# A sparse-expert decoder block: interleaved columns and a VectorE turn for the rest rows, another order at the first block, and no loads for further blocks where there are none

## The chip, the cores and the metric

The kernel runs on one core of one Trainium2 chip. The metric is the device time of one execution in microseconds (us). Three executions of the kernel before took 2183.55, 2186.32 and 2188.81 us.

## The reference, cut to what matters

One decoder block over 1024 tokens of width 1024: two attention mixers, an output projection, then a sparse FFN with 32 experts. Each token goes to 4 experts, so an expert has 128 tokens on average. The change lies in the FFN alone.

```
logits = xf @ router_w + router_b;  top 4 of 32;  gate = softmax(top logits)
for each expert e, over its tokens x (rows of RMSNorm(h)):
    gu  = x @ w_gate_up[e] + b_gate_up[e]            # 1024 -> 2048, fp32
    g   = min(gu[:, :1024], 7);  u = clip(gu[:, 1024:], -7, 7)
    act = (u + 1) * (g * sigmoid(1.702 * g))
    out[token] += (act @ w_down[e] + b_down[e]) * gate
```

## The kernel before, in words

**Stages.** Norm and attention come first, then merge and output projection with routing, then `experts` (from L1870 on), which computes block b for expert b, b = 0 to 31. A block holds up to 160 token rows. The first 128 are the main rows, the 32 behind them the rest rows. An expert with more than 160 tokens gets further blocks (number 32 and on), whose number `nov` is known only on the chip (`further_blocks`, L1958).

**Main rows.** The weights of a block come in 12 slabs of 1 MB (8 of gate and up, 4 of down), issued by SyncE. ScalarE writes the rounded part `w_hi` of each slab (`split_hi`, L2031), VectorE the remainder `w_lo` (`split_lo`, L2298), and TensorE multiplies hi by hi, lo by hi and hi by lo (`gate_up` L2446, `down` L2490). Half of the hidden columns is ready after slab 3, the other after slab 7. They are activated by ScalarE (`swish`) and VectorE (`activate`), turned on TensorE (`turn_hidden`, L2406), and split by ScalarE (`hidden_hi`) and VectorE (`hidden_lo`, L2329).

**Rest rows.** They are multiplied only in an expert with more than 128 tokens (`more` in `multiply`). With 32 rows a product fills only a quarter of TensorE's columns, so four column groups g = 0 to 3 work side by side, each on another quarter of the output columns, in plain fp32 out of the raw slab (`gate_up_rest` L2468, `down_rest` L2507). In PSUM, partitions 32g to 32g+31 hold the 32 rows for the hidden columns of quarter g: 128 adjoining columns of each half. ScalarE and VectorE activate this tile in every block (`swish_rest` L2043, `activate_rest` L2320 and L2322). In a block with rest rows TensorE then turns the two 128x128 tiles (`turn_hidden_rest`, L2414), between slabs 9 and 10, and ScalarE copies the turned tile to `h_rest` (`hidden_rest`, L2056; in every block). `down_rest` reads `h_rest` behind slab 10.

**Rows in and out.** While block b runs, POOL copies the index tables of block b+2 and, once VectorE has turned the rows of block b+1, gathers the rows of block b+2 by five indirect DMAs (`gather`, L2141). VectorE turns them (`turn_x`, `turn_x_rest` L2348), and ScalarE and VectorE split them (`take_x`, L2065 and L2357). At the end of a block ScalarE scales the result (`take_y` L2071, 128x1024; `take_y_rest` L2078, 128x256), and POOL adds both to the output in HBM by an indirect DMA each (`add_rows`, L2148 main, L2151 rest). On POOL the order in a block is: `add_rows(b-1)`, the new index tables, then the gather. For a further block the tables are read back from `slots` in HBM by 25 small DMAs (`load_slots`, L2131 to L2136).

**The two ends of the stage.** At the start VectorE waits for an iota of POOL (`ini`, L2360), runs `split_lo(0, 0)`, and only then turns the gathered rows of block 0 (L2364), which `take_x(0)` needs. At the end VectorE and ScalarE split three slabs of a block 32 and turn its rows, and POOL loads the tables of blocks 32 and 33 and gathers their rows, whether `nov` is above 0 or not; `add_rows(31)` is behind all of this on POOL.

```
turn = pe.wait(hid2_d); transpose(gu[:, 1, 1, a*P:(a+1)*P], hid2[:, a, :], ident)   # a = 0, 1  (L2410 on)
more:  main(8) turn_hidden(1) main(9) turn_hidden_rest main(10) down_rest(8..11) main(11)
```

## Time and profile before

| | |
|---|---|
| three executions | 2183.55, 2186.32, 2188.81 us (median 2186.32) |
| the profiled execution | 2186.8 us, its span 2185.2 us |
| mean granted TensorE clock | 0.985 |
| TensorE busy | 2095.8 us, 96% of the span |
| VectorE, ScalarE, POOL busy | 1609.1, 1323.1, 850.5 us |
| `w_hi` and `w_lo` splits | 387 each: 32 blocks of 12 slabs and 3 more |

The span runs from the first to the last instruction of the core; the profiled execution's own time is 1.6 us longer. A block without rest rows takes about 34.4 us, one with them 46.5 us. 18 of the 32 blocks have rest rows. 387 splits are 32 blocks of 12 and the three that are made ahead for block 32: on this input no further block runs.

### The profile page before, as it was taken

The numbers are of one execution on the slowest core, as the hardware profiler recorded it, in microseconds if no ns is written. First come the engines' busy times: TensorE is split into PE (matmuls) and PEld (weight loads), VectorE is DVE, ScalarE is ACT, GpSimd is POOL, SyncE is SP. The second block draws the span as 40 slices with busy tenths as digits, with TensorE's granted clock in tenths as the row PEclk, the third lists the DMA queues.
The fourth block names the chain that finished last, engine by engine and source line by source line (L and its number), as shares of the span: only waits on it lengthen the run. The fifth ranks groups of instructions, "written<-read, shape, count | busy, mean of one in ns | idle before, by whom it ended". The sixth has DMA issues, their size and how long they took to land.

```text
span 2185.2 us, 38817 instructions
## 1 busy us (share of the span) xinstructions
PE 2095.8 (96%) x13480; PEld 1618.2 (74%) x13481; DVE 1609.1 (74%) x1604; ACT 1323.1 (61%) x1463; POOL 850.5 (39%) x698
## 2 busy tenths in 40 slices
PE   7989999999999997999999999999999999999995
PEld 7867777777777775777777777777887777777774
DVE  4165767676666466897897897898998778777885
ACT  4266675756444224676676676676876566665664
POOL 1120101010066344465665653454645334433376
PEclk9999999999999997999999999999999999999997
DMA  4101212122255538899999998999999899888992
GB/s 154 31 29 46 70 36 71 29 63 62 78 174 195 190 128 299 310 345 331 336 355 340 332 353 314 346 363 350 396 362 366 280 337 333 309 282 304 345 318 69
DMA packets 270040, 515.19 MB, mean 236 GB/s; under 512 B 37733, under 2 KB 80176, under 8 KB 269964
## 3 DMA queue, kind: packets, MB, share of 16 engines
q1 hardware_dynamic: 242308, 469.61, 59.7%
q0 software_dynamic: 20000, 39.16, 7.3%
q10 hardware_dynamic: 7656, 5.44, 0.8%
q8 instruction: 44, 0.72, 0.1%
q14 instruction: 32, 0.26, 0.0%
HBM read 475.83 MB, written 42.45 MB: 237 GB/s over the span
## 4 chain that ended last, share of the span: by engine, by line
PE 55%; POOL 3%; DVE 1%; issue 1%; DMA 1%; ACT 0%; POOLq 0%; DVEq 0%; ACTq 0%
PE ex_gu L2446 30%; PE ex_yp L2490 15%; PE ex_rest L2468 6%; PE ex_rest L2507 3%; POOL ex_xg L2141 1%; POOL ex_nxt_q L2136 1%; DVE ex_wlo L2298 1%; PE ex_tr L2406 1%; PE ex_gu L2406 1%; DMA out_dram<-ex_ytok,ex_piece 1%; PE ex_gu L2433 0%; DMA ex_nxt_q<-slots 0%; POOL out_dram L2148 0%; PE ex_yp L2437 0%; POOL ex_idx L2171 0%
## 5 line engine op out<-in xcount | busy, mean ns | idle before, releaser
L2298 DVE TENSOR_TENSOR ex_wlo<-ex_raw,ex_whi 128x2048 fp32r<-128x2048 f32 x387 | 872.9, 2286 | 138.6 <-ACT ex_whi L2031 132.5
L2031 ACT ACTIVATE ex_whi<-ex_raw 128x2048 fp32r<-128x2048 f32 x387 | 731.5, 1913 | 133.7 <-PE ex_gu L2446 115.0
L2141 POOL DMA_INDIRECT ex_xg<-xn_s,ex_idx x165 | 338.5, 2052 | 400.6 <-DVE ex_xrest L2348 346.8
L2446 PE MATMUL ex_gu<-ex_whi,ex_xhi 128*128 128x512 f32 x1024 | 284.9, 400 | 13.3 <-DVE ex_xlo L2357 13.1
L2446 PE MATMUL ex_gu<-ex_whi,ex_xlo 128*128 128x512 f32 x1024 | 275.5, 391 | 0.0
L2446 PE MATMUL ex_gu<-ex_wlo,ex_xhi 128*128 128x512 f32 x1024 | 274.5, 390 | 0.0
L2446 PEld LDWEIGHTS ex_gu<-ex_whi,ex_xhi 128*128 128x128 f32 x1024 | 186.4, 189 | 69.2 <-issue 21.6
L2446 PEld LDWEIGHTS ex_gu<-ex_whi,ex_xlo 128*128 128x128 f32 x1024 | 192.9, 188 | 41.6
L2446 PEld LDWEIGHTS ex_gu<-ex_wlo,ex_xhi 128*128 128x128 f32 x1024 | 192.6, 188 | 41.1
L742 POOL TENSOR_TENSOR at_wlo<-at_raw,at_whi 128x1024 fp32r<-128x1024 f32 x15 | 36.1, 2404 | 451.4 <-ACT at_whi L555 451.4
L58 PE MATMUL at_job<-xnT_hi,at_whi 128*128 128x512 f32 x416 | 178.6, 429 | 5.2 <-DVE at_nxt_qa L778 2.9
L60 PE MATMUL at_job<-xnT_hi,at_wlo 128*128 128x512 f32 x416 | 164.3, 395 | 0.0
L59 PE MATMUL at_job<-xnT_lo,at_whi 128*128 128x512 f32 x416 | 163.6, 393 | 0.0
L2490 PE MATMUL ex_yp<-ex_whi,ex_hhi 128*128 128x512 f32 x512 | 147.0, 409 | 0.0
L2490 PE MATMUL ex_yp<-ex_whi,ex_hlo 128*128 128x512 f32 x512 | 137.8, 391 | 0.0
L2490 PE MATMUL ex_yp<-ex_wlo,ex_hhi 128*128 128x512 f32 x512 | 137.7, 391 | 0.0
L2468 PE MATMUL ex_rest<-ex_raw,ex_xrest 128*32 128x256 f32 x2304 | 135.7, 381 | 0.0
L2490 PEld LDWEIGHTS ex_yp<-ex_whi,ex_hlo 128*128 128x128 f32 x512 | 96.2, 188 | 21.5
L2490 PEld LDWEIGHTS ex_yp<-ex_wlo,ex_hhi 128*128 128x128 f32 x512 | 96.2, 188 | 21.3
L2490 PEld LDWEIGHTS ex_yp<-ex_whi,ex_hhi 128*128 128x128 f32 x512 | 89.7, 188 | 28.9 <-issue 11.1
L2468 PEld LDWEIGHTS ex_rest<-ex_raw,ex_xrest 128*32 128x32 f32 x2304 | 70.5, 110 | 53.3 <-issue 12.7
L643 ACT ACTIVATE at_probT<-at_tr 128x512 f32<-128x512 f32 (+1 forms) x120 | 63.2, 527 | 75.9 <-PE at_tr L1022 75.7
(379 smaller groups left out, 3494.6 us busy)
## 6 DMA issues: line engine op xcount, KB each, us to landing
ex_raw<-in_w_gate_up_dram SPq DMA_DIRECT2D x512, 512.0 KB, 8.3
ex_raw<-in_w_down_dram SPq DMA_DIRECT2D x256, 512.0 KB, 8.0
at_raw<-in_w_in_dram SPq DMA_DIRECT2D x25, 512.0 KB
gT<-at_gst SPq DMA_DIRECT2D x32, 256.0 KB, 2.3
mg_g<-gT SPq DMA_DIRECT2D x32, 256.0 KB, 3.9
raw_o<-in_w_out_dram SPq DMA_DIRECT2D x8, 512.0 KB, 5.6
op_x<-in_x_dram SPq DMA_DIRECT2D x8, 512.0 KB, 4.1
out_dram<-op_h SPq DMA_DIRECT2D x8, 512.0 KB, 2.8
```

What stands on the lines that cost most here:

```text
L58: nc.tensor.matmul(out, w_hi, x_hi, start=first, stop=False)
L59: nc.tensor.matmul(out, w_hi, x_lo, start=False, stop=False)
L60: return nc.tensor.matmul(out, w_lo, x_hi, start=False, stop=last)
L643: nc.scalar.activation(probT[:, slot(u), 4 * g:4 * g + n, :].rearrange("p a c -> p (a c)"), tr[:, 0:n * P], ACT.Copy).then_inc(tr_ev, 1)
L2031: nc.scalar.activation(w_hi[:, i % RING, :], raw[:, i % SLABS, :], ACT.Copy).then_inc(hi_d, 1)
L2141: pool.indirect_dma_start(out=xg[:, a, :], out_offset=None, in_=xn_s.rearrange("t (q c) -> (t q) c", q=Q), in_offset=bass.IndirectOffsetOn ...
L2298: nc.vector.tensor_tensor(w_lo[:, slot, :], raw[:, i % SLABS, :], w_hi[:, slot, :].bitcast(F32), ALU.subtract).then_inc(lo_d, 1)
L2406: last = nc.tensor.transpose(dst[:, k * P:(k + 1) * P], hid[:, (4 * half + k) * P:(4 * half + k + 1) * P], ident[:, :])
L2446: mm = nc.tensor.matmul(gu[:, half, h, :], x[:, k, :], w[:, kk, h, :], start=half == 0 and k == 0 and n == 0, stop=k == KD - 1 and n == 2)
L2468: mm = nc.tensor.matmul(part(g), x_rest[:, k, :], gate_up_slab(raw, i)[:, kk, :, g * P:(g + 1) * P], start=k == 0, stop=k == KD - 1)
L2490: mm = nc.tensor.matmul(yp[:, nh, :], x[:, k, :], w[:, kk, nh * HALF:(nh + 1) * HALF], start=False, stop=k == KD - 1 and n == 2)
L2507: mm = nc.tensor.matmul(part(g), h_rest[:, k, :], down_slab(raw, i)[:, kk, g * XW:(g + 1) * XW], start=k == 0, stop=k == KD - 1)
```

## The change

- **Rest rows.** The column groups take interleaved columns. Group g reads, of every 128 columns, the 32 from 32g on: 8 runs of 32 floats for each product of 256 columns, where it read 2 runs of 128. Then each 32x32 piece of `hid2` turned in its place is a piece of `h_rest`. VectorE does that with one transpose of 128x256, in every block, behind `activate_rest`. TensorE's `turn_hidden_rest` and ScalarE's `hidden_rest` are gone, and `down_rest` waits for VectorE.
- **First block.** VectorE no longer waits for `ini`. It turns the gathered rows and does `take_x(0)` before `split_lo(0, 0)`, `split_lo(0, 1)` and the turn of the rest rows.
- **Further blocks.** The rows, tables and slab splits for block 32 are prepared inside `If(nov > 0)` (`begin_further`). The last block prepares nothing.
- **Last output.** The last `take_y` is shared: ScalarE takes columns 0 to 511, VectorE 512 to 1023. `add_rows` issues the rest rows' DMA first, before it waits for the main rows.

The diff, cut to its core:

```diff
@@ further_blocks
+        def further_blocks(eng, body, begin=None):
             with eng.If(nov > 0):
+                if begin is not None:
+                    begin()
@@ scalar
-            def hidden_rest(b):
-                act.wait_ge(h_tr, 3 * b + 3)
-                src = gu[:, 1, 1, 0:2 * P].rearrange("p (k c) -> p k c", k=KD)
-                nc.scalar.activation(h_rest[:, :, :], src, ACT.Copy).then_inc(hh_d, 1)
+            def take_y_half(b):
+                act.wait_ge(slab_mm, SLABS * b + SLABS + RING)
+                act.wait_ge(cur_d, b + 1)
+                nc.scalar.activation(ytok[:, 0:HALF], yp[:, 0, :], ACT.Copy, scale=cur[:, 0, 1:2].bitcast(F32)).then_inc(y_ev, 1)
                 hidden_hi(b, 1)
-                take_x(b + 1)
-                hidden_rest(b)
-                for i in range(12, SLABS + AHEAD):
-                    split_hi(b, i)
+                if not last:
+                    take_x(b + 1)
+                    for i in range(12, SLABS + AHEAD):
+                        split_hi(b, i)
-            body(NE - 1, True)
-            nov = further_blocks(act, body)
-            take_y(nov + (NE - 1))
+            body(NE - 1, False, last=True)
+            nov = further_blocks(act, body, begin_further)
+            take_y_half(nov + (NE - 1))
@@ gpsimd
-            def add_rows(b):
-                hold(pool, y_ev, b + 2, spare)
+            def add_rows(b, parts=1):
                 hold(pool, y2_ev, b + 2, spare)
...
+                hold(pool, y_ev, b + 1 + parts, spare)
...
+            def begin_further():
+                pool.wait_ge(tok_out, 16 * NT * TOPK)
+                next_rows(NE, on_chip=False, late=1)
+                advance(NE + 1)
+                next_rows(NE + 1, on_chip=False)
@@ vector
                 nc.vector.scalar_tensor_tensor(out=hid2[:, :, :], in0=sg2[:, :, :], scalar=SWISH_CAP, in1=hid2[:, :, :],
                                                op0=ALU.min, op1=ALU.mult).then_inc(hid2_d, 1)
+                dve.wait_ge(hid2_d, 2 * b + 2)
+                nc.vector.transpose(h_rest[:, :, :], hid2[:, :, :].rearrange("p a (k c) -> p (a k) c", c=CAP2)).then_inc(hid2_d, 1)
-            dve.wait_ge(ini, 1)
-            split_lo(0, 0)
             for a in range(Q):
                 dve.wait_ge(*landed[max(a - 1, 0)])
                 last = nc.vector.transpose(x_t[:, :, a * CAP2:(a + 1) * CAP2], pieces[:, :, a, :])
             last.then_inc(x_tr, 2)
             take_x(0)
+            for i in range(2):
+                split_lo(0, i)
             dve.wait_ge(*landed[Q - 1])
             turn_x_rest(0)
+            def take_y_half(b):
+                dve.wait_ge(slab_mm, SLABS * b + SLABS + RING)
+                dve.wait_ge(cur_d, b + 1)
+                nc.vector.tensor_scalar(ytok[:, HALF:D], yp[:, 1, :], cur[:, 0, 1:2].bitcast(F32), None, ALU.mult).then_inc(y_ev, 1)
@@ tensor
-            def turn_hidden_rest(b):
-                pe.wait_ge(hid2_d, b + 2)
-                for a in range(2):
-                    last = nc.tensor.transpose(gu[:, 1, 1, a * P:(a + 1) * P], hid2[:, a, :], ident[:, :])
-                last.then_inc(h_tr, 1)
+                his = lambda w, g: w.rearrange("p h (n q c) -> p h n q c", q=Q, c=CAP2)[:, :, :, g, :]
                         mm = nc.tensor.matmul(part(g), x_rest[:, k, :],
-                                              gate_up_slab(raw, i)[:, kk, :, g * P:(g + 1) * P],
+                                              his(gate_up_slab(raw, i)[:, kk, :, :], g),
                 if i == 8:
-                    pe.wait_ge(hh_d, 3 * b + 6)
+                    pe.wait_ge(hid2_d, 2 * b + 3)
                 main(9)
-                if more:
-                    turn_hidden_rest(b)
                 main(10)
```

## Rows read from the trace of the kernel before

**Rows 1.** The page, part 1: busy time by engine.

```profile
PE 2095.8 (96%) x13480; PEld 1618.2 (74%) x13481; DVE 1609.1 (74%) x1604; ACT 1323.1 (61%) x1463; POOL 850.5 (39%) x698
```

**Rows 2.** Waits on TensorE from 900 to 2165 us: total, times, longest (us).

```profile
PE ex_tr L2406 <- DVE ex_hid L2312: 0.9, 1, 0.9
```

**Rows 3.** Timeline at the start of the expert stage: start, length (us), instruction.

```profile
829.29 0.94 POOL L2141 DMA_INDIRECT ex_xg<-xn_s,ex_rows_of  x1 [0.30 <-issue]
...
831.96 2.29 DVE L2298 TENSOR_TENSOR ex_wlo<-ex_raw,ex_whi 128x2048 fp32r<-128x2048 f32 x1 [6.11 <-POOL ex_iota L2187]
...
834.17 1.42 DVE L2364 STREAM_TRANSPOSE ex_hid<-ex_xg 128x256 f32<-128x256 f32 x4
...
835.62 1.15 ACT L2065 ACTIVATE ex_xhi<-ex_hid 128x512 fp32r<-128x512 f32 x2 [11.01 <-DVE ex_hid L2364]
...
837.63 2.07 PE L2446 MATMUL ex_gu<-ex_whi,ex_xhi 128*128 128x512 f32 x4 [13.10 <-DVE ex_xlo L2357]
```

**Rows 4.** The gathered tile from 820 to 840 us: from a DMA's issue to its landing.

```profile
DMA to landing us min/median/max: 2.7/2.7/2.7
```

**Rows 5.** Windows: stretch, length, busy by engine, then granted clock, DMA share, GB/s.

```profile
837.00:842.00 5.00, 4.37 (x11) 3.47 (x12) 4.33 (x4) 5.00 (x3) 3.63 (x4) 0.54 0.85 277
```

**Rows 6.** TensorE's timeline around the turn of the rest rows, block from 1952 us on.

```profile
1987.98 1.08 PE L2490 MATMUL ex_yp<-ex_wlo,ex_hhi 128*128 128x512 f32 x4
1988.90 0.38 PE L2414 MATMUL ex_gu<-ident,ex_hid 128*128 128x128 f32 x2
...
1990.97 1.07 PE L2490 MATMUL ex_yp<-ex_wlo,ex_hhi 128*128 128x512 f32 x4
```

**Rows 7.** Groups by line on TensorE, 837.6 to 2161 us: busy, mean ns, idle before.

```profile
L2414 PE MATMUL ex_gu<-ident,ex_hid 128*128 128x128 f32 x36 | 6.9, 273 | 0.0
```

**Rows 8.** TensorE's timeline, same block: half a gate-up rest stretch, and the down rest stretch.

```profile
1963.79 1.93 PE L2468 MATMUL ex_rest<-ex_raw,ex_xrest 128*32 128x256 f32 x32
...
1967.49 1.20 PE L2446 MATMUL ex_gu<-ex_whi,ex_xhi 128*128 128x512 f32 x4
...
1991.96 0.64 PE L2507 MATMUL ex_rest<-ex_raw,ex_hrest 128*32 128x256 f32 x8
...
1995.66 1.20 PE L2490 MATMUL ex_yp<-ex_whi,ex_hhi 128*128 128x512 f32 x4
```

**Rows 9.** VectorE's timeline in a block without rest rows, from 1604.35 us on.

```profile
1627.43 0.69 DVE L2308 TENSOR_SCALAR ex_hid<-ex_gu 128x512 f32<-128x512 f32 x1 [0.31 <-PE ex_gu L2446]
1628.37 0.69 DVE L2312 SCALAR_TENSOR_TENSOR ex_hid<-ex_sg,ex_hid 128x512 f32<-128x512 f32 x1 [0.24 <-ACT ex_sg L2037]
...
1633.79 0.41 DVE L2348 STREAM_TRANSPOSE ex_xrest<-ex_xg 128x256 f32<-128x256 f32 x1
...
1637.49 6.70 DVE L2298 TENSOR_TENSOR ex_wlo<-ex_raw,ex_whi 128x2048 fp32r<-128x2048 f32 x3
```

**Rows 10.** TensorE's timeline, the first product of the next block that reads `w_lo`.

```profile
1640.55 1.07 PE L2446 MATMUL ex_gu<-ex_wlo,ex_xhi 128*128 128x512 f32 x4
```

**Rows 11.** Timeline of the end.

```profile
2159.39 1.07 PE L2490 MATMUL ex_yp<-ex_wlo,ex_hhi 128*128 128x512 f32 x4
...
2161.95 1.11 ACT L2071 ACTIVATE ex_ytok<-ex_yp,ex_cur 128x1024 f32<-128x1024 f32 x1
...
2171.99 1.64 POOL L2148 DMA_INDIRECT out_dram<-ex_ytok,ex_cur  x1 [0.30 <-issue]
2173.93 1.60 POOL L2151 DMA_INDIRECT out_dram<-ex_ytok,ex_piece  x1 [0.30 <-issue]
```

**Rows 12.** L2148, then L2151, from 2165 us on: from issue to landing.

```profile
DMA to landing us min/median/max: 5.9/5.9/5.9
...
DMA to landing us min/median/max: 4.3/4.3/4.3
```

**Rows 13.** Timeline at the end of block 0: `take_y`, then the add it releases.

```profile
893.28 1.10 ACT L2071 ACTIVATE ex_ytok<-ex_yp,ex_cur 128x1024 f32<-128x1024 f32 x1
...
895.44 1.77 POOL L2148 DMA_INDIRECT out_dram<-ex_ytok,ex_cur  x1 [6.63 <-issue]
```

More of the change, by code:

```diff
@@ L2084, in _, with body @@
                 split_hi(0, i)
-            def body(b, last, first=False):
+            def body(b, over, first=False, last=False):
                 split_hi(b, AHEAD)
@@ L2101, in body @@
                 hidden_hi(b, 1)
-                take_x(b + 1)
-                hidden_rest(b)
-                for i in range(12, SLABS + AHEAD):
-                    split_hi(b, i)
                 if not last:
+                    take_x(b + 1)
+                if not last:
+                    for i in range(12, SLABS + AHEAD):
+                        split_hi(b, i)
+                if not last and not over:
                     act.wait_ge(raw_mm, SLABS * b + 10)
@@ L2109, in body @@
                 take_y_rest(b)
+            def begin_further():
+                take_x(NE)
+                for i in range(12, SLABS + AHEAD):
+                    split_hi(NE - 1, i)
             body(0, False, first=True)
@@ L2161, in next_rows @@
                 hold(pool, idx_d, 3 * b - 2, spare)
+            def next_rows(b, on_chip=True, late=0):
                 if on_chip:
@@ L2215, in body, with begin_further @@
                     scatter(t)
+                near_end = isinstance(b, int) and b >= NE - 2
+                if near_end and b == NE - 1:
+                    hold(pool, idx_d, 3 * b + 2, spare)
+                    return
                 hold(pool, idx_d, 3 * b + 3, spare)
-                if isinstance(b, int) and b == NE - 2:
-                    pool.wait_ge(tok_out, 16 * NT * TOPK)
-                next_rows(b + 2, on_chip=not over and (not isinstance(b, int) or b + 2 < NE))
+                advance(b + 2)
+                if not near_end:
+                    next_rows(b + 2, on_chip=not over)
+            def begin_further():
+                pool.wait_ge(tok_out, 16 * NT * TOPK)
+                next_rows(NE, on_chip=False, late=1)
+                advance(NE + 1)
+                next_rows(NE + 1, on_chip=False)
             for b in range(2 + NT):
@@ L2305, in activate @@
                 dve.wait_ge(hid_d, n + 1)
-                after(dve, h_tr, 3 * b + half - 2)
+                after(dve, h_tr, 2 * b + half - 1)
                 us = hid[:, half * HALF:(half + 1) * HALF]
@@ L2366, in _, with body @@
             take_x(0)
+            for i in range(2):
+                split_lo(0, i)
             dve.wait_ge(*landed[Q - 1])
             turn_x_rest(0)
-            for i in range(1, AHEAD):
+            for i in range(2, AHEAD):
                 split_lo(0, i)
-            def body(b, over):
+            def body(b, over, last=False):
                 for i in range(AHEAD, 7):
@@ L2383, in body, with begin_further @@
                 hidden_lo(b, 1)
-                turn_x(b + 1, 0)
-                turn_x(b + 1, 1)
-                turn_x_rest(b + 1)
+                if not last:
+                    turn_x(b + 1, 0)
+                    turn_x(b + 1, 1)
+                    turn_x_rest(b + 1)
                 split_lo(b, 11)
-                take_x(b + 1)
-                for i in range(12, SLABS + AHEAD):
-                    split_lo(b, i)
+                if not last:
+                    take_x(b + 1)
+                    for i in range(12, SLABS + AHEAD):
+                        split_lo(b, i)
+            def begin_further():
+                turn_x(NE, 0)
+                turn_x(NE, 1)
+                turn_x_rest(NE)
+                take_x(NE)
+                for i in range(12, SLABS + AHEAD):
+                    split_lo(NE - 1, i)
+            def take_y_half(b):
+                dve.wait_ge(slab_mm, SLABS * b + SLABS + RING)
+                dve.wait_ge(cur_d, b + 1)
+                nc.vector.tensor_scalar(ytok[:, HALF:D], yp[:, 1, :], cur[:, 0, 1:2].bitcast(F32), None, ALU.mult).then_inc(y_ev, 1)
             body(0, False)
@@ L2394, in _ @@
             destinations()
-            over_blocks(dve, body, first=2)
+            with dve.Fori(2, NE - 1) as b:
+                body(b, False)
+            body(NE - 1, False, last=True)
+            nov = further_blocks(dve, body, begin_further)
+            take_y_half(nov + (NE - 1))
         @block.tensor
@@ L2399, in _, with turn_hidden @@
             pe.sem_inc(slab_mm, RING)
-            def turn_hidden(b, half, alone=False):
+            def turn_hidden(b, half):
                 pe.wait_ge(hid_d, 2 * b + half + 2)
@@ L2459, in gate_up_rest @@
                 if pair_of_k == 2:
+                    pieces = bias[:, 0:2 * FF].rearrange("p (h c) -> p h c", h=2)[:, :, half * HALF:(half + 1) * HALF]
                     for g in range(Q):
[L2461 to L2464 removed]
+                        nc.tensor.matmul(part(g), ones_first[:, :], his(pieces, g), start=False, stop=False)
                 for kk in range(2):
@@ L2529, in multiply @@
                 main(8)
-                turn_hidden(b, 1, alone=not more)
+                turn_hidden(b, 1)
                 main(9)
-                if more:
-                    turn_hidden_rest(b)
                 main(10)
```

43 lines of the change are left out of this document (19 added, 24 removed).

## The prediction

> **What bounds the kernel now.** I read the page's busy shares first: TensorE is busy for 96% of the span and VectorE for 74% [rows 1]. The reader should see that an average over the stages settles nothing for the others, so I went to the waits on TensorE alone. From 900 to 2165 us, nearly the whole expert stage, its longest wait is 0.9 us [rows 2]. So inside the expert stage only TensorE's own work counts, as long as no helper falls behind. What is left is at the two ends of the stage, and I read both as timelines. At the start TensorE stands for 13.1 us, released by VectorE [rows 3]. At the end the last product is over at 2159.39 + 1.07 = 2160.5, and the adds to the output are issued only at 2172.0 and 2173.9 [rows 11]: POOL gathers rows for a block that never runs in between.
>
> **The change part by part.**
>
> *Start.* VectorE waited for POOL's iota, ran a split of 2.29 us and only then turned the gathered rows, from 834.17 to 835.59 [rows 3]. The fourth gather is issued at 829.29 [rows 3] and lands 2.7 us later [rows 4], at 832.0. In the new order three of the four turns are done by then and the last takes about 0.4 us (a quarter of the 1.42 us, with its start-up), so it ends at 832.4 instead of 835.6. What follows (x_hi, x_lo, first product at 837.63) moves with it: 3.2 us. The two splits of 2.29 us moved behind `take_x` are hidden: `w_lo` of slab 0 is done some 4.3 us after the turn, TensorE starts 2.0 us after it and has two products of 1.9 us or so to do first at its low clock. The turn of the rest rows comes about 2 us later in absolute time, and with it POOL's gather for block 1, which has most of block 0 (46 us) as cover. One thing may be given back. In 837 to 842 us the granted clock was 0.54 [rows 5], that is 1.2 GHz nearly to 842, after 13 us in which TensorE stood, and then it rose. If the rise kept its place in time, 3.2 us more of work would run at half speed, a loss of 1.6; if it came as long after the start as now, none. I take 0.5. **Start: -2.7 us** (-1.6 to -3.2).
>
> *Turn of the rest rows off TensorE.* 36 matmuls of 273 ns [rows 7], two for each of 18 blocks. They are pipelined, so their duration isn't their price. A product of four matmuls starts 0.92 us after the one before (1987.98 to 1988.90). From the turn at 1988.90 to the third product at 1990.97 are 2.07 us for the turn and two products [rows 6], so the turn costs 2.07 - 1.84 = 0.23, or 0.26 against products at 0.91. I take 0.25 x 18. **-4.5 us** (at most -9.8, if every one of the 36 counted in full; at least 0, if another gap takes its place, rival 3). By the Trainium skill, "TensorE: Matmul & The Clock Gate", PE-mode transpose, one transpose takes about 390 ns in isolation and about 275 ns in one kernel's context. An estimate from the former would give 14 us for 36. The row agrees with the second figure in duration, and its neighbours show that most of it overlaps.
>
> `down_rest` now waits for VectorE. Between the second half's rest stretch and `down_rest` TensorE works on slabs 8, 9 and 10, nine products of 0.92 = 8.3 us [rows 6]; less under 2 us for the activation, 6 us cover one transpose. ScalarE loses a copy of 128x256 in every block; it isn't late anywhere, so nothing.
>
> *Turn on VectorE.* It is paid in all 32 blocks, also in the 14 without rest rows, where VectorE has hardly any room. The nearest row is the turn of another 128x256 tile in the same engine and direction: 0.41 us [rows 9]. It also has to wait for the full end of the operation before it, which now overlaps its successor by some 0.08, so the shift is 0.45. In the block without rest rows VectorE's only idle stretches are 0.31 and 0.24 us, both around activating the second half [rows 9]: 0.55 together. So 0.45 is absorbed there, block by block, with 0.10 over. Between the turn and that place everything on VectorE is 0.45 later. The tightest reader is the first `w_lo` of the next block: split from 1637.49, three in 6.70, the first done at 1639.8, wanted by TensorE at 1640.55 [rows 9, 10]. The 0.75 shrink to 0.3. Cost: **0 us** (bounds: nothing, and 14 x 0.4 = 6 if the turn took twice the row; a gain is excluded, as VectorE only gets more to do). By the Trainium skill, "VectorE: DVE Perf Modes", The three transpose paths, VectorE needs 311 ns for 128x128 in bf16. An estimate from that, 0.62 us for 128x256, would exceed the 0.55. The measured row is for the very shape and type, so I go by it.
>
> *Interleaved columns.* The number of products, their columns and their output layout in PSUM are unchanged; only the moving operand is read in 8 runs of 32 floats instead of 2 of 128. No row shows runs of 32. The nearest rows compare runs of 128 with one run of 256: half a gate-up stretch takes 1967.49 - 1963.79 = 3.70 us, the down stretch of as many products 1995.66 - 1991.96 = 3.70 [rows 8]. Halving the run cost nothing, so I take **0 us**. The stretches it touches are 2 x 18 x 3.70 = 133 us, so each per cent would be 1.3 us; the far end is a doubling, +133. A gain is excluded by the same two rows.
>
> *End.* The loads, gathers, splits and row turns for block 32 go, and POOL waits at `add_rows(31)`. ScalarE isn't behind three splits, so the rest part is ready at about 2160.3 (released inside the last product, then a copy under half of the 1.11 us in rows 11). From a release to the issue of an add I take 895.44 - 894.38 = 1.06 us [rows 13]. The rest DMA is issued at 2161.4 and takes 1.60 + 0.30 [rows 11]. The main DMA follows at 2163.3; its data, in halves on ScalarE and VectorE (0.6 to 0.7 us each), is ready at 2161.2, so that sharing is hidden behind the rest DMA. It lands 5.9 us after its issue [rows 12], at 2169.2. Now the two land at 2171.99 + 5.9 = 2177.9 and 2173.93 + 4.3 = 2178.2 [rows 11, 12], and the span ends at 2185.2, 7.0 us later. With the same 7.0 the new end is 2176.2. **-9.0 us** (-7.0 if the way past the code of the further blocks or a slower issue costs 2 us; -10.9 if the order of the two DMAs cost nothing). TensorE is not concerned: its last block never waited for this.
>
> **The sum:** -2.7 - 4.5 + 0 + 0 - 9.0 = -16.2 us against the profiled execution's 2186.8, so 2170.6. That execution lies 0.5 above the median of 2186.32, so against the median 2170.1.
>
> **The rivals.** 0.2% of the time is 4.4 us, about what a measurement of this kernel can tell from no change.
>
> 1. *The interleaved read slows the rest products.* For: no row has such short runs, and four column groups read at once. Against: 256 against 128 makes no difference [rows 8]. The sign turns at 16.2 / 133 = 12% per product. At a quarter more each, +33: about 2203 us, slower. Chance 7%.
> 2. *VectorE becomes the bound in blocks without rest rows.* For: 0.10 us is all that is left [rows 9], and several such blocks follow one another. Against: the measured turn. With a turn of 0.6 to 0.9 us, 0.1 to 0.4 x 14, so 1.5 to 6 us given back: 2172 to 2176. Chance 15%; the skill's figure named above points here.
> 3. *The turn on TensorE was free,* and its 0.25 turns up as a longer gap elsewhere, or the end gains only 7: 2172 to 2175. Chance 13%.
> 4. *The change doesn't do what it says.* If further blocks ran, the end would still be prepared in full, only later, with -2.7 - 4.5 left: 2179. The 387 splits, 32 x 12 + 3, say none do. Chance 1%.
>
> **How the numbers follow.** My forecast, every term within its bounds: 64%, 2170. The range takes it in with the end at -10.9 and the start at -3.2, a little over 2 us better, plus some 1.5 for where a median of three falls: 2166. Upward it takes in rivals 2 and 3: 2176. It leaves out rival 1 and the extremes. Faster by over 0.2% (below 2181.9): forecast, rivals 2, 3, and 4: 92%. Within 0.2%: a slowing of 9 to 16% in rival 1, 3%. Slower: 5%.
>
> **What the profile after would show.** First products at about 834.5 and not 837.6. No L2414 rows, and about 46.2 us for a block with rest rows against 46.5. In blocks without rest rows still 34.4 us, VectorE's idle time before the second half's activation down to about 0.1, and no wait of TensorE on `w_lo`. The half stretches of the rest rows still 3.70 us. No gather or table load behind 2125 us, the two adds issued some 1 us and 3 us after the last product, and 7 us from the last landing to the end. A mean above 381 ns for the rest products, or a TensorE wait on `w_lo` in runs of plain blocks, would prove it wrong.

## The result, and the profile after

The changed kernel takes 2164.17 us, the median of 2162.26, 2164.03, 2164.31 and 2168.24. The kernel before, run beside it, takes 2185.65 us (four runs, 2183.55 to 2188.81). The ratio is 0.9903, 95% interval 0.9884 to 0.9922. So it is faster, as forecast, but by 21.5 us where the prediction had 16.2: the median lies 1.8 us below the low end of the range.

The profiled execution after is the slowest of the four, 2168.24 us. The page of the changed kernel, its span and part 1, against [rows 1]:

```profile
span 2166.6 us, 38402 instructions
...
PE 2092.8 (97%) x13444; PEld 1613.0 (74%) x13445; DVE 1619.8 (75%) x1629; ACT 1308.1 (60%) x1426; POOL 823.8 (38%) x635
```

TensorE has the 36 instructions of `turn_hidden_rest` less and is busy 3.0 us less, while the span fell by 18.6 us. So the gain is mostly not in TensorE's work. A table of four stretches, each read from TensorE's timeline, shows where it lies. The stage is taken to begin with the small products that bring the slot rows (822.66 before, 824.02 after).

| stretch, us | before | after | gain |
|---|---|---|---|
| slot rows to the first expert product | 14.97 | 11.97 | 3.0 |
| first product to block 0's bias products | 10.48 | 10.07 | 0.4 |
| bias products of block 0 to those of block 31 | 1286.28 | 1283.81 | 2.5 |
| last matmul to the end of the span | 25.04 | 10.98 | 14.1 |

Bias products are the small products that add a block's biases; they come once in each block, so the time from one block's to the next's is the length of a block. From block 31's bias products to the last matmul both kernels take 25.7 us, and the last stretch counts from that last matmul's start. The stretches give 19.9 us. All that lies ahead of the stage took 1.4 us more after, in code that the change doesn't touch, which leaves the 18.6 us of the spans.

**Start.** The timeline of the changed kernel at the start of the stage, against [rows 3]:

```profile
833.50 0.45 DVE L2390 STREAM_TRANSPOSE ex_hid<-ex_xg 128x256 f32<-128x256 f32 x1 [0.81 <-DMA ex_xg<-xn_s,ex_rows_of]
833.98 1.15 ACT L2061 ACTIVATE ex_xhi<-ex_hid 128x512 fp32r<-128x512 f32 x2 [8.01 <-DVE ex_hid L2390]
835.86 4.49 DVE L2325 TENSOR_TENSOR ex_wlo<-ex_raw,ex_whi 128x2048 fp32r<-128x2048 f32 x2
835.99 2.07 PE L2489 MATMUL ex_gu<-ex_whi,ex_xhi 128*128 128x512 f32 x4 [10.11 <-DVE ex_xlo L2385]
```

VectorE now turns each gathered piece as it lands and has the last one done at 833.95, 9.9 us behind the slot rows. Before, a split ended at 834.25 with four turns behind it, the last done at 835.59, 12.9 us behind the slot rows. The split of slab 0 is behind `take_x` (at 835.86, in one row with slab 1's).

**Blocks.** TensorE's timeline in a block with rest rows of the changed kernel: half a gate-up rest stretch, and what follows it, against [rows 8].

```profile
979.62 1.93 PE L2510 MATMUL ex_rest<-ex_raw,ex_xrest 128*32 128x256 f32 x32
...
983.32 1.20 PE L2489 MATMUL ex_gu<-ex_whi,ex_xhi 128*128 128x512 f32 x4
```

That is 3.70 us again, with 8 runs of 32 floats where there were 2 of 128: the interleaved read costs nothing. The page's group of these products says so for the whole kernel, 380 ns each (381 before):

```profile
L2510 PE MATMUL ex_rest<-ex_raw,ex_xrest 128*32 128x256 f32 x2304 | 135.7, 380 | 0.0
```

From bias products to bias products, a block with rest rows takes 46.23 us (46.49 before), 0.26 less; only blocks 0 and 1 (46.55 and 47.3) stay as they were: the turn's 0.24 us is gained at its place there too, but the bias products of the block behind it wait for ScalarE's `take_y` that much longer (0.25 us where there was no wait before, and 1.01 instead of 0.75). The 18 blocks with rest rows give 4.05 us together. The 13 without them, of blocks 0 to 30, take 1.57 us more: block 2 went from 35.91 to 36.42, the others from 34.39 to between 34.39 and 34.56. So 2.5 us arrive.

**End.** The timeline of the end, against [rows 11]:

```profile
2154.88 1.07 PE L2532 MATMUL ex_yp<-ex_wlo,ex_hhi 128*128 128x512 f32 x4
...
2156.08 0.75 DVE L2435 TENSOR_SCALAR ex_ytok<-ex_yp,ex_cur 128x512 f32<-128x512 f32 x1 [3.90 <-PE ex_yp L2532]
2156.41 0.69 ACT L2074 ACTIVATE ex_ytok<-ex_yp,ex_cur 128x512 f32<-128x512 f32 x1 [0.64 <-PE ex_yp L2532]
2156.68 1.57 POOL L2157 DMA_INDIRECT out_dram<-ex_ytok,ex_piece  x1 [21.84 <-ACT ex_ytok L2080]
2158.56 1.56 POOL L2162 DMA_INDIRECT out_dram<-ex_ytok,ex_cur  x1 [0.30 <-issue]
```

The issues of the adds start 0.7 and 2.6 us after the last product is over (2154.88 + 1.07 = 2155.95); foretold were 0.9 and 2.8. Counted from the start of its last matmul, as in the table and in all that follows, it is 1.1 and 3.0 us. The tile `out_dram`, line L2162, from issue to landing: 6.0 us, against 5.9 in [rows 12].

```profile
DMA to landing us min/median/max: 6.0/6.0/6.0
```

So the last landing is at 2164.6, 8.6 us behind the last product (foretold 8.7), and the span ends 2.0 us later. Before, that distance was 6.9 us, by when SP sees the landing (the prediction's 7.0 comes from 2173.93 + 4.3 = 2178.2, the span's end being 2185.2), and the prediction kept it. Line L1886 is the end of the stage's program: SP goes through it once the output has landed, POOL stays in its DRAIN. Before:

```profile
L1886 POOLq DRAIN  x1: 16070/16070/16070, 2168.9 to 2168.9; - x1
L1886 SPq DRAIN  x1: 7/7/7, 2178.3 to 2178.3; - x1
```

After:

```profile
L1886 POOLq DRAIN  x1: 8425/8425/8425, 2157.9 to 2157.9; - x1
L1886 SPq DRAIN  x1: 7/7/7, 2164.6 to 2164.6; - x1
```

The first figure is the duration in ns. POOL's queue runs ahead, so its DRAIN starts before the last issues are over; it is its end that counts. POOL's drain ended at 2185.0 before, 6.7 us behind the landing, and at 2166.3 after, 1.7 behind it.

### The profile page after: what moved, and what is told of

It reads as the page before. It is cut to its first block, busy times and chain, and to the rows that moved or that the text cites. A ratio compares the mean times of both kernels' runs of the same rounds, so it can differ in the third digit from the quotient of the medians.

```text
span 2166.6 us, 38402 instructions
## 1 busy us (share of the span) xinstructions
PE 2092.8 (97%) x13444; PEld 1613.0 (74%) x13445; DVE 1619.8 (75%) x1629; ACT 1308.1 (60%) x1426; POOL 823.8 (38%) x635
## 4 chain that ended last, share of the span: by engine, by line
PE 59%; DVE 2%; issue 1%; ACT 0%; POOL 0%; DMA 0%; POOLq 0%; ACTq 0%; DVEq 0%
PE ex_gu L2489 32%; PE ex_yp L2532 16%; PE ex_rest L2510 6%; PE ex_rest L2549 3%; DVE ex_wlo L2325 1%; PE ex_gu L2456 1%; PE ex_tr L2456 1%; PE ex_gu L2476 0%; PE ex_yp L2480 0%; ACT ex_whi L2033 0%; PE ex_rest L2506 0%; POOL ex_xg L2151 0%; DMA ex_xg<-xn_s,ex_rows_of 0%; DVE ex_hid L2369 0%; DVE ex_xlo L2385 0%
## 5 line engine op out<-in xcount | busy, mean ns | idle before, releaser
L2151 POOL DMA_INDIRECT ex_xg<-xn_s,ex_idx x155 | 322.4, 2080 | 343.0 <-DVE ex_xrest L2376 292.7
L2489 PE MATMUL ex_gu<-ex_whi,ex_xhi 128*128 128x512 f32 x1024 | 285.7, 401 | 10.8 <-DVE ex_xlo L2385 10.1
L2222 POOL COPY ex_cur<-ex_mid 128x4 int32<-128x4 int32 x32 | 37.0, 1155 | 218.0 <-DMA out_dram<-ex_ytok,ex_cur 218.0
```

The source lines that it names most:

```text
L2151: pool.indirect_dma_start(out=xg[:, a, :], out_offset=None, in_=xn_s.rearrange("t (q c) -> (t q) c", q=Q), in_offset=bass.IndirectOffsetOn ...
L2222: nc.gpsimd.tensor_copy(cur[:, :, :], mid[:, :, :]).then_inc(cur_d, 1)
L2489: mm = nc.tensor.matmul(gu[:, half, h, :], x[:, k, :], w[:, kk, h, :], start=half == 0 and k == 0 and n == 0, stop=k == KD - 1 and n == 2)
```

## The experiments

The diffs are cut to the lines that matter. The kernels of the first group below (`no_end`, `no_start`, `no_rest`), `xrest_later` and the two at the very end were timed several times, the others once; a single time can't tell 2 us, so those are read by stretches of their traces.

Two theories on the end stood at first. **The drain**: the 4.9 us not foretold lie in POOL's drain, which takes longer after the loads and gathers that the old end issued. **The order**: they come from the order of the two adds (another one lands last). The recorded expectations have letters of their own: for `no_end`, A is the fixed 7.0 us and B the drain; for `order_back` and the gathers, P is the drain and O the order. On the blocks: the 1.6 us lost in the blocks without rest rows come from VectorE's new turn, or from nothing but scatter.

### Each part undone alone

`no_end` puts back the preparation of block 32, the single `take_y` and the old order of the adds:

```diff
-            nov = further_blocks(pool, body, begin_further)
-            add_rows(nov + (NE - 1), parts=2)
+            nov = further_blocks(pool, body)
+            add_rows(nov + (NE - 1))
```

> The changed kernel with its end undone: the tables, gathers, row turns and splits for a block 32 are made as before, the adds go main rows first, and ScalarE alone scales the last result. Theory A (the end closes a fixed 7.0 us after the last landing, as predicted): 9 us slower than the changed kernel, about 2173. Theory B (the end closes with the drain on POOL, which takes longer when five gathers lie just ahead of the adds: 9.4 us behind the last issue in the profile before, 6.2 us in the one after): 14 us slower, about 2178, and a drain that ends 9.4 us after the last add's issue ends.

Measured: 2180.64 us, ratio to the kernel before 0.9984 (0.9974 to 0.9993). Its timeline on POOL:

```profile
2164.94 0.95 POOL L2151 DMA_INDIRECT ex_xg<-xn_s,ex_idx  x1 [0.30 <-issue]
2166.20 1.64 POOL L2158 DMA_INDIRECT out_dram<-ex_ytok,ex_cur  x1 [0.30 <-issue]
2168.14 1.60 POOL L2161 DMA_INDIRECT out_dram<-ex_ytok,ex_piece  x1 [0.30 <-issue]
```

Start and blocks keep their gain (11.94 and 1283.72 us), but the adds come 13.6 and 15.5 us after the last product, 11.9 and 13.9 in the kernel before: POOL's loads and gathers end the kernel, and don't move up fully when TensorE does. From the last matmul to the end it takes 26.70 us. The drain ends 9.4 us behind the last issue, as the drain theory has it; the order isn't excluded yet. Without the end part the other two are worth 3.5 us: they save 5.6 by its trace, and the old end gives 1.7 of it back (26.70 against 25.04). The end part on top of them is worth 15.7 us by the trace and 16.5 by the medians, more than the 14.1 of the table by what the old end would have given back.

`no_start` puts `ini` and `split_lo(0, 0)` ahead of the turns again:

```diff
+            dve.wait_ge(ini, 1)
+            split_lo(0, 0)
             for a in range(Q):
```

> The changed kernel with the old order at the first block (wait for the iota, split of slab 0, then the turns). Theory (prediction): first product 3.0 to 3.2 us later, counted from the end of the routing stage, so about 3 us slower than the changed kernel, 2167. Rival (other work at the start is late next, so that block 0 gives the gain back): under 1 us.

Measured: 2167.52 us, ratio 0.9929 (0.9912 to 0.9945); 14.98 us to the first product, with blocks (1283.90) and end (11.04) as in the changed kernel. The part is worth 3.0 us by the trace, as expected, and block 0 doesn't give it back.

`no_rest` puts back adjoining columns, TensorE's turn and ScalarE's copy:

```diff
-                nc.vector.transpose(h_rest[:, :, :], hid2[:, :, :].rearrange("p a (k c) -> p (a k) c", c=CAP2)).then_inc(hid2_d, 1)
+            def turn_hidden_rest(b):
+                pe.wait_ge(hid2_d, b + 2)
+                for a in range(2):
+                    last = nc.tensor.transpose(gu[:, 1, 1, a * P:(a + 1) * P], hid2[:, a, :], ident[:, :])
```

> The changed kernel with the rest rows handled as before: adjoining columns, two turns on TensorE, a copy on ScalarE, no transpose on VectorE. Theory A (prediction, VectorE's transpose is hidden): blocks with rest rows 46.49 us, those without 34.39, and 4.5 us slower in all. Theory B (the transpose delays slab 11's w_lo, and with it the first product of the next block, by 0.1 us in most blocks without rest rows, and blocks 0 and 2 wait for something else): every block without rest rows back at 34.39, and only 2.5 us slower in all.

Measured: 2169.45 us, ratio 0.993 (0.9914 to 0.9947); blocks 1286.39 us. So the rest part is worth 2.6 us, the whole of what the blocks gained. From block 3 on the blocks without rest rows are back at 34.39 and those with rest rows at 46.49, and block 2 is back at 35.91: Theory B of the expectation came, so the loss in the blocks without rest rows is the change's and not scatter.

### VectorE's turn, doubled and made room for

`turn_twice` adds a second transpose of the same size in every block, into a tile nobody reads:

```diff
+                nc.vector.transpose(sg2[:, :, :].rearrange("p a (k c) -> p (a k) c", c=CAP2), hid2[:, :, :].rearrange("p a (k c) -> p (a k) c", c=CAP2))
```

> The changed kernel with one more transpose of 128x256 on VectorE in every block, just before the one that turns the rest rows. It prices the place: VectorE has been left 0.1 us short in blocks without rest rows. Theory B (slab 11's w_lo is the last thing TensorE waits for there, nothing has room behind it): each of the 14 blocks without rest rows grows by about the whole 0.4 us, to 34.9 us, about 5 us in all; blocks with rest rows stay at 46.23. Rival (the slack is elsewhere and the 0.1 us was all): 34.5 us as now.

Measured: 2170.46 us; blocks 1287.79 us, 4.0 more than the changed kernel, 3.85 of it in the 13 blocks without rest rows (36.72 for block 2, 34.66 to 34.86 for the others). About 5 had been expected, 0.4 a block. VectorE's timeline behind block 4 (without rest rows), then TensorE's:

```profile
1040.40 0.45 DVE L2351 STREAM_TRANSPOSE ex_sg<-ex_hid 128x256 f32<-128x256 f32 x1
1040.77 0.40 DVE L2352 STREAM_TRANSPOSE ex_hrest<-ex_hid 128x256 f32<-128x256 f32 x1
...
1043.21 2.25 DVE L2325 TENSOR_TENSOR ex_wlo<-ex_raw,ex_whi 128x2048 fp32r<-128x2048 f32 x1
1045.38 1.28 DVE L2386 TENSOR_TENSOR ex_xlo<-ex_hid,ex_xhi 128x512 fp32r<-128x512 f32 x2
```

```profile
1046.15 1.07 PE L2533 MATMUL ex_yp<-ex_wlo,ex_hhi 128*128 128x512 f32 x4
1047.38 1.19 PE L2490 MATMUL ex_gu<-ex_whi,ex_xhi 128*128 128x512 f32 x4 [0.16 <-ACT ex_whi L2033]
```

The wait is at the change of blocks: 1.23 us between two starts where 0.91 is the rhythm. The profile puts it down to ScalarE's `w_hi`, but the one that the product needs was ready at 1045.43. What fits is slab 11's `w_lo`: it is done at 1045.46, and the next block's first product starts 1.92 us behind it. The changed kernel has the same distance behind the same block (1044.33 and 2.25 is 1046.58):

```profile
1044.33 2.25 DVE L2325 TENSOR_TENSOR ex_wlo<-ex_raw,ex_whi 128x2048 fp32r<-128x2048 f32 x1
1046.50 1.28 DVE L2385 TENSOR_TENSOR ex_xlo<-ex_hid,ex_xhi 128x512 fp32r<-128x512 f32 x2
```

```profile
1047.60 1.07 PE L2532 MATMUL ex_yp<-ex_wlo,ex_hhi 128*128 128x512 f32 x4
1048.51 1.19 PE L2489 MATMUL ex_gu<-ex_whi,ex_xhi 128*128 128x512 f32 x4
```

In the kernel before it was 2.37 us and the product was 1.07 long. The room was 0.45 us (2.37 less 1.92), and one transpose of 0.45 uses it up: 1.93 is left, and the first product is 0.12 longer. The second transpose then costs about 0.3 us a block. Behind block 2 there was no room even before (1.87 us, with a wait of 0.16), so that block pays the first transpose in full, 0.5 us.

What fills these 1.92 us is in the trace: TensorE's own queue. The branches around it (L2598) and the load of the next block's count into a register (L2597), from 1046 to 1048.6 us in the changed kernel:

```profile
L2598 PEldq COMPARE_BRANCH  x2: 177/194/212, 1046.6 to 1048.0; - x2
L2597 PEldq TENSOR_LOAD <-rt_loads x1: 307/307/307, 1047.3 to 1047.3; - x1
```

The same lines of the kernel before, from 1047.5 to 1050.3 us:

```profile
L2558 PEldq COMPARE_BRANCH  x2: 173/192/212, 1048.0 to 1049.3; - x2
L2557 PEldq TENSOR_LOAD <-rt_loads x1: 303/303/303, 1048.7 to 1048.7; - x1
```

The first branch starts 0.06 us behind the end of slab 11's `w_lo`, behind every block without rest rows of both kernels, of `turn_twice`, `no_rest`, `xrest_later` and `both_orders`. So this queue waits for that `w_lo`, and not for `w_hi`, which in the kernel before ends 0.2 us after the branch has started. From the first of these instructions to the last it takes 1.8 us where the next block has rest rows and 1.65 where it has none. Wherever the product starts late at the change of blocks, in `turn_twice` behind all 13, the last of them ends 0.06 us ahead of it; before, it was 0.5 us ahead where the next block has rest rows and 0.65 where it has none. This also sorts the loss in the changed kernel: 0.09 to 0.17 us in the eight blocks that have one with rest rows behind them, 0.03 at most in the four that don't (and 0.5 in block 2).

`xrest_later` moves the turn of the next block's rest rows behind slab 11's split:

```diff
-                    turn_x_rest(b + 1)
                 split_lo(b, 11)
                 if not last:
+                    turn_x_rest(b + 1)
                     take_x(b + 1)
```

> The changed kernel, with VectorE's turn of the next block's rest rows (0.33 us from start to start) moved behind the split of slab 11. Theory B (the first product of the next block waits on the chain slab 11's w_lo, then TensorE's last product, register load and branch): all blocks without rest rows fall from 34.5 to 34.39, 1.2 us in all. Rival (what is waited for is x_lo of the next block, which doesn't move): they stay at 34.5.

Measured: blocks 1282.57 us, 1.24 less than the changed kernel, and all blocks without rest rows at 34.39 again, but for block 2 (36.12). The time is 2165.09 us, ratio 0.9917 (0.99 to 0.9933), not to be told from the changed kernel's: 1.2 us is less than the runs can show, so this gain is read from the trace alone. `x_lo`, which the next block's first product waits for too, is no later or earlier for the move, yet the loss is gone. And the one change of blocks in this kernel with a wait left, at 962.69, has slab 11's `w_lo` 1.93 us ahead and `x_lo` 0.40 ahead, where `x_lo` is 0.72 ahead in the changed kernel: it is the distance to `w_lo` that stays the same. So Theory B of the expectation came, and the rival (`x_lo`) did not.

### The end: what the drain takes

`order_back` issues the main rows' add first again:

```diff
+                hold(pool, y_ev, b + 1 + parts, spare)
                 hold(pool, y2_ev, b + 2, spare)
+                pool.indirect_dma_start(out=out[0, :, :], ...
                 pool.indirect_dma_start(out=out.rearrange("a t (q c) -> (a t q) c", q=Q),
```

> The changed kernel, but its adds wait for both parts and issue the main rows' DMA first, the rest rows' second. D is the time from the end of the last add's issue to the end of POOL's drain: 9.4 us in the kernel before, 6.2 us in the changed one. Theory P (gathers just ahead in POOL's queue lengthen the drain): D stays 6.2 us. Theory O (the order of the two adds sets it, a last DMA with small rows drains slowly): D is 9.4 us.

Measured: 2166.06 us; last matmul to end 10.86 us (10.98 changed), end of the span 1.98 us behind the landing in both. The order theory falls: the order makes 0.1 us of difference and not 4.9. What the earlier landing of the last add saves, its later issue takes.

`gathers_early` and `gathers_late` issue five gathers (into tiles nobody reads) ahead of the last adds, the second of these kernels only when the rest rows' result is there (its diff is shown); `gather_late1` issues one there:

```diff
+            hold(pool, x_tr, 3 * NE, spare)
+            hold(pool, y2_ev, nov + (NE + 1), spare)
+            gather(lambda a: idx[:, a:a + 1])
             add_rows(nov + (NE - 1), parts=2)
```

> The changed kernel with five more gathers on POOL behind block 30's add, as soon as it is free, some 20 us before the last adds. (They write rows that nothing reads.) Theory P1 (only what is still in POOL's queue when the adds are issued counts): D 6.2 us and the span as in the changed kernel. Theory P2 (each DMA issued since some earlier point counts, landed or not): D 9.4 us. Theory O: D 6.2 us.

> The changed kernel with five more gathers directly ahead of the last two adds, behind the wait for the rest rows' result. Theories P1 and P2: D 9.4 us, and the gathers' issue, 5 x 1.25 = 6.3 us, ahead of it: last product to end of span 11.1 + 6.3 + 3.2 = 20.6 us. Theory O: D 6.2, so 17.4 us.

> As with five gathers directly ahead of the adds, but one. If the drain grows with the number of DMAs ahead, 3.2 / 5 = 0.64 us each: D 6.9 us. If one is enough for the whole of it: D 9.4 us. If it isn't the gathers: 6.2 us.

Measured: 2169.09, 2170.64 and 2167.68 us; the span ends 2.19, 2.19 and 2.02 us behind the landing, against 1.98. Five gathers add 0.2 us to that distance, one gather 0.04, and how late they are changes nothing. That is the drain theory's sign but not its size: the expectation for five late gathers was a drain that ends 9.4 us behind the last issue, and it ends at 6.4 (6.5 with the early ones).

`loads20_end` and `loads50_end` issue 20 and 50 of the small table loads there instead, `loads20_mid` issues 20 of them some 900 us earlier:

```diff
             nov = further_blocks(pool, body, begin_further)
+            extra_loads(20)
             add_rows(nov + (NE - 1), parts=2)
```

> The changed kernel with 20 small table loads (32 rows of 8 bytes each, as those of load_slots, into a tile nobody reads) on POOL behind block 30's add, before the last two adds. The gathers tried add little to the time from the last landing to the end (2.0 us without, 2.2 us with five, wherever they lie), so what made it 6.9 us is open. Theory L (each small table load adds to it, 4.9 us less 0.4 for ten gathers, over 50 loads, so 0.09 us each): 3.8 us. Rival (it is something else in the kernel before, as the code for the further blocks or the work on the other engines): 2.0 us.

> The same with 50 loads, waiting for them after each 20. Theory L: 6.5 us from the last landing to the end. Rival: 2.0 us. The adds themselves come later here, since the loads' issue (0.5 us each) runs past the last product; only the time behind the landing is compared.

> The same 20 loads, but behind block 9 on POOL, some 900 us before the end. If POOL's last drain works off what it has issued in the whole run: 3.8 us from the last landing to the end, as with 20 at the end. If only the recent ones count: 2.0 us.

Measured: 2166.05, 2180.01 and 2164.88 us. The span ends 2.80, 4.43 and 1.74 us behind the landing. So what is issued near the end counts, for each DMA, and what is long past does not (why it is 0.24 us less than without these loads stays open). Both sizes were missed: 3.8 and 6.5 were expected if the loads are the cause, 2.0 if not. Line L1886 of `loads50_end`:

```profile
L1886 POOLq DRAIN  x1: 11725/11725/11725, 2166.4 to 2166.4; - x1
L1886 SPq DRAIN  x1: 7/7/7, 2174.0 to 2174.0; - x1
```

`end_no_loads` is `no_end` without the 50 loads (it takes the rows of block 31 again; ten gathers stay). `end_rest_first` is `no_end` with the new order of the adds. `loads50_gathers10` is `loads50_end` with ten gathers more, that is all 60 DMAs of the old end in another order and place:

```diff
-                    load_slots(b)
+                    nc.gpsimd.tensor_copy(idx[:, :], rows_of[:, :, NE - 1:NE].rearrange("p a o -> p (a o)"))\
+                        .then_inc(idx_d, 1)
```

```diff
+            extra_loads(50)
+            for a in range(2):
+                gather(lambda a: idx[:, a:a + 1])
```

> The changed kernel with its end undone, as in the first call, but without the 50 table loads (the ten gathers for blocks 32 and 33 take the rows of block 31 again; nothing reads them). Each small load or gather of POOL added 0.04 to 0.05 us to the time from the last landing to the end; 60 of them give 2.5 to 3 us, but the kernel before has 4.9 more than the changed one. Theory N (the loads are all of it, at 0.09 each in this place): 1.98 + 0.4 = 2.4 us from the last landing to the end. Theory M (0.05 for each DMA, and 2 us from something else in the old end): 2.4 + 2 = 4.4 us.

> The changed kernel with its end undone but the new order of the two adds. If the order is the something else: 6.7 - 2 = 4.7 us from the last landing to the end. If only the landing moves (main rows' DMA 1.6 us later): the landing comes 1.6 us later, and the end moves less or not at all if the drain had been busy for other reasons (D 9.4 us as before), or by the same 1.6 us if the work starts with the landing (6.7 us behind it, D 11).

> The changed kernel with all 50 loads and ten gathers of the old end put ahead of its last adds, and none of the rest of the old end. Theory N (what POOL issued near the end is all of it): 6.9 us from the last landing to the end. Theory M: 1.98 + 2.45 + 0.4 = 4.8 us.

Measured: 2168.49, 2180.9 and 2196.71 us. `loads50_gathers10` stays at 5.10 us from landing to end, where 6.9 was expected if the DMAs are all of it; the table below has why. Its line L1886:

```profile
L1886 POOLq DRAIN  x1: 12228/12228/12228, 2182.6 to 2182.6; - x1
L1886 SPq DRAIN  x1: 7/7/7, 2190.0 to 2190.0; - x1
```

And `end_rest_first`:

```profile
L1886 POOLq DRAIN  x1: 15013/15013/15013, 2164.0 to 2164.0; - x1
L1886 SPq DRAIN  x1: 7/7/7, 2174.2 to 2174.2; - x1
```

Two distances now sort all of these kernels: from the landing, as SP sees it, to the end of the span, and from the end of the last add's issue to the end of the drain. "Further" DMAs are those that the changed kernel doesn't have.

| kernel | further DMAs by POOL near the end | landing to end of span | last issue to end of drain |
|---|---|---|---|
| before | 60 | 6.86 | 9.40 |
| no_end | 60 | 6.70 | 9.40 |
| end_rest_first | 60 | 5.06 | 9.40 |
| loads50_gathers10 | 60 | 5.10 | 9.40 |
| loads50_end | 50 | 4.43 | 8.58 |
| end_no_loads | 10 | 2.65 | 5.31 |
| loads20_end | 20 | 2.80 | 7.07 |
| gathers_early | 5 | 2.19 | 6.53 |
| gathers_late | 5 | 2.19 | 6.41 |
| gather_late1 | 1 | 2.02 | 6.33 |
| changed | 0 | 1.98 | 6.24 |
| order_back | 0 | 1.98 | 4.62 |
| loads20_mid | 0 (20 some 900 us earlier) | 1.74 | 6.00 |

With 60 such DMAs the drain ends 9.40 us after the last issue, in four kernels whose landings differ by 1.8 us: there it does not wait for the landing. With 50 (all loads) it is 8.58, with 10 (all gathers) it is 5.31: 0.082 us for each, load or gather. Continued to none it would be 4.5, an estimate that no kernel shows, as there the landing is later. In the rows from `loads20_end` on the landing comes too late for the count to matter, and the drain ends 1.7 us behind it (the span 2.0), 0.04 us more for each DMA. So two limits, of which the later one counts, fit all the rows but the 0.24 us of `loads20_mid`. The old end was bound by the count, the new one by the landing. `end_rest_first` beside `no_end` also shows again that the order isn't the cause: 9.40 with either. What POOL does for each DMA in its drain no row shows; that stays open, as does how far back a DMA counts: the old end issued its 60 over some 75 us ahead of the last add, and 900 us are too far.

### Once more, and both orders

`after_again` is the changed kernel. `both_orders` is the changed kernel with the edits of `xrest_later` and `order_back`:

```diff
                     turn_x(b + 1, 1)
-                    turn_x_rest(b + 1)
                 split_lo(b, 11)
                 if not last:
+                    turn_x_rest(b + 1)
```

> The changed kernel, unchanged, timed again. By the stretches of the profiles it should be 3.0 (start) + 2.5 (blocks) + 14.1 (end) = 19.6 us faster than the kernel before: ratio 0.991. A ratio of 0.9926 or more would put the prediction's 16.2 us right after all.

> The changed kernel with the turn of the next block's rest rows behind the split of slab 11 (1.2 us less in the blocks, by the profile) and the main rows' add issued first again (0.1 to 0.3 us less at the end). 21 us faster than the kernel before, ratio 0.9904; against the changed kernel 1.4 us, which is less than one timing can tell, so the stretches of the profile decide: blocks 1282.6 us from the first bias product to the last, and at most 10.9 us from the last product to the end.

Measured: 2164.89 us (2162.66 to 2169.26), ratio 0.9901 (0.9884 to 0.9917), and 2166.11 us (2163.61 to 2166.47), ratio 0.9906 (0.9889 to 0.9923). The second has shorter blocks (1282.59) and a shorter end (10.80) than the changed kernel, 1.4 us together, and the runs don't show it. The changed kernel repeats itself, its stretches within 0.05 us (11.98, 1283.83, 11.03), and its 21 us against the kernel before rule out the 16.2 (a ratio of 0.9926, outside the interval).

Why 1.4 us doesn't show: in the traces the slot rows come between 817.3 and 824.2 us, in code that is the same in all kernels. Ahead of them TensorE's granted clock falls to the lower level in short stretches, in different places from execution to execution. From 60 us on they make 3.4 us in all where the slot rows come at 817.3, and 17 us where they come at 823.5 to 824.2: half a us is lost for each us at half the clock. Both profiled executions of the changed kernel have 17 us of them, the one of the kernel before has 14. That moves whole executions by more than these edits do, so small edits are judged by stretches of the trace.

## Why the prediction was right or wrong

- **The end: the mechanism was right, a term was wrong.** The prediction gave 9.0 us, "with the same 7.0" from the last landing to the end. The measured gain is 14.1. The adds start and land as foretold, within 0.2 us. The step that failed is the 7.0, taken over as a constant: 4.9 of it came with the 60 DMAs that POOL had issued near the end, and it fell to 2.0. This alone is 4.9 of the 5.3 us by which the gain was missed. The bounds (7 to 10.9) held the 7.0 fixed at both ends, so the range left no room for it. A row that might have warned was in the trace of before: POOL's drain of 16.07 us, of which 6.7 lie behind the landing, with nothing on any engine in between.
- **The start: right.** 2.7 foretold within 1.6 to 3.2, 3.0 measured, `no_start` confirms it. The 0.5 us held back for the clock were not lost: the stretch behind the first product gained 0.4, which would put the term at 3.4, above its bound. The windows of the changed kernel, against [rows 5], have the granted clock behind the busy times: 0.54 in the first 3.4 us, 1.2 GHz for nearly all of them, and full (2.4 GHz) behind them. Before, the 0.54 of 837 to 842 puts the rise at about 841.6, 4 us behind the first product. This stretch varies from 10.1 to 11.0 us among kernels with the same code there, so the 0.4 can't be put down to the change.

```profile
836.00:839.40 3.40, 3.40 (x9) 2.68 (x10) 3.40 (x2) 3.40 (x3) 2.58 (x9) 0.54 0.88 257
839.40:842.00 2.60, 2.60 (x13) 2.16 (x12) 2.60 (x3) 1.70 (x2) 2.44 (x3) 1.00 0.76 221
```

- **The turn off TensorE: right in size.** 4.5 foretold for 18 blocks, 4.05 measured: 0.26 in each of 16, nothing in blocks 0 and 1, where `take_y` is waited for. By the page "TensorE: Matmul & The Clock Gate" of the Trainium skill (Part 4: PE-mode transpose), whose figure for a transpose alone is 390 ns, for bf16, the prediction had worked out some 14 us as an estimate; the 273 ns of [rows 7] was the better guide, and even that is more than the path gave back, since a pair of turns took 0.26 us of it.
- **VectorE's turn at nothing: wrong, by 1.6 us.** The prediction said that 0.10 us would be left over and that the reader with the least room was the next block's `w_lo`. It missed the reader with less: slab 11's own `w_lo`, behind which TensorE's queue has 1.65 to 1.8 us of its own work before the next block's first product. The waits of before ([rows 2]) don't show this but for 0.2 us in block 2, because it was met everywhere else, by 0.4 to 0.6 us. The prediction's own sign of being wrong, blocks without rest rows above 34.4, came. Rival 2 (VectorE becomes the bound in blocks without rest rows) held in part: at this place, and for up to 0.17 us a block (0.5 in block 2), not as an engine that is full.
- **The transpose itself** was 0.45 us for 128x256, near the 0.41 of [rows 9].
- **Interleaved columns at nothing: right**, 3.70 us a stretch; Rival 1 did not come. **Rival 3** (the turn was free, or the end gains only 7 us) did not come either: `no_rest` and `no_end` show both parts at work. **Rival 4** did not: every part does what it says.
- **The sum.** Foretold 16.2 us: 2.7, 4.5, 0 and 9.0. Profiled: 3.4, 4.05, 1.6 against it, and 14.1, less 1.4 for what lies ahead of the stage, 18.6 in all; the medians of the runs give 21.5, since the profiled execution after was the slowest of its four. So but for the end the misses nearly cancel, which is luck: 0.7 at the start and 2.9 from the choice of executions one way, 0.45, 1.6 and 1.4 the other.

## What to carry to other kernels

The time from the last landing to the end is not a constant: if POOL issues DMAs near the end, look at its DRAIN. In this kernel, where that ended long after the landing, every DMA taken out was worth about 0.08 us besides its issue, until the landing itself became the limit. Before calling a new instruction on a side engine free, check every reader behind it for room, and count for the last reader of a loop body what its queue still has to do before the next pass begins. A gain below the scatter of the runs can still be read from a trace, by the distance between two fixed instructions on either side of the edit.

## What was not expected of the hardware

- POOL's final drain grows with the number of DMAs it issued in the last 75 us or so: from the end of the last issue to the drain's end 5.31 us for 10 further ones, 8.58 for 50, 9.40 for 60, 0.082 us each, wherever the last landing falls before that. 20 DMAs 900 us earlier add nothing.
- The moving operand of a product in 8 runs of 32 floats is as fast as in 2 runs of 128: 380 and 381 ns.
- From the end of what TensorE's queue waits for last in a block (slab 11's `w_lo`) to the next block's first product it takes 1.74 to 1.93 us, though the product between takes 0.9: the queue's branches and its register load (0.3 us) fill it.
- The part of the kernel ahead of this stage takes 817.3 to 824.2 us from one execution to the next, half a us more for each us that it spends at the lower clock, 3.4 to 17 us in all.
